# Where a modulation's weights are multiplied: 24 units of layer 1 move from the first block's heads to three norms of the second block

## The chip, the core and the metric

One core of a Trainium2 chip runs the whole program, in one launch. The metric is the device time of that launch in microseconds, as a median of runs. TensorE (PE) multiplies, VectorE (DVE) and ScalarE (ACT) do element-wise work on SBUF and PSUM, GpSimd (POOL) does one kind of subtraction here, and SyncE (SP) issues the loads of the weights.

## The reference, cut to what matters

Two transformer blocks of two layers each work on 256 tokens of width 1024, all in f32. The second block modulates its normed input by vectors that depend on a condition `c` alone:

```
mod_lat = silu(c) @ ada_w[l] + ada_b[l]          # 6 * 1024 columns
mod_ctx = silu(c_ctx) @ ada_w[l] + ada_b[l]
sh1, sc1, g1, sh2, sc2, g2 = split(mod, 6)
h = rmsnorm(x, norm1_g) * (1 + sc1) + sh1        # then mixer, then
x = x + g1 * out;  h2 = rmsnorm(x, norm2_g) * (1 + sc2) + sh2
x = x + g2 * conv_ffn(h2)
```

`ada_w` is two matrices of 1024 x 6144. Nothing in them waits for the first block, so their products can be made anywhere before the layer that uses them. The first block's attention has 24 heads (three mixers of eight) in each layer. The second block runs a context stream and a latent stream: layer 0 on the context, the keys and values of layer 1 on the context, then layers 0 and 1 on the latents.

## The kernel before, in words

All weights come as one stream of 908 units of 128 x 1024 f32 (512 KB), in the order in which PE uses them. `stream()` writes this order. SP loads unit i into one of seven `raw` buffers (L553) once unit i - 7 has left it. For an ordinary (split) unit ACT copies `raw` to a rounded `whi` (L1270, four buffers, a buffer is free when PE has used the unit four split units earlier), POOL computes the rest `wlo` (L568), and PE multiplies high by high, high by low and low by high (L599, L600, L603, or L616, L651 to L655 and L781 in other forms). A plain unit holds a 128-column tile of `ada_w` and isn't split: PE reads `raw` itself (L827) and the `raw` buffer is free when PE is done with it. Every engine walks the same stream by its own counter. ACT's counter runs four stream positions ahead of PE's, plain positions included; at a plain position `hi_part` does nothing.

`modulation_tile` (L827) multiplies one plain unit: eight f32 matmuls, each in two passes, whose 32-row outputs stand in four column groups of PE. The rows belong to the two conditions.

The 96 tiles of the two `ada_w` are spread over the first block. Of each layer's 48, 24 stand in `first_layer` beside the 24 heads, two ahead of the scores of each of the twelve pairs of heads (`pair_scores`). There DVE adds each tile's result to a running row in `lowest`, and twice a layer a matmul with a selecting matrix (L838, `modulation_columns`) turns twelve tiles' rows into columns and DVE adds the bias. The other 24 stand in three groups of eight in the layer's cross attention and in its two layer norms: there the eight accumulate in one PSUM tile of `lin`, ACT copies it once (`mod_row`), one L838 turns it (`unit_columns`) and `unit_bias` on DVE stores it and frees `lin` half 1. In the norms they lie between the small matmuls of the norm (`norm_with_modulation`), the last two in the chunk behind it (`columns_behind`).

Between the heads of a pair PE runs units of other projections (`first_fill`; `BEFORE_PV`, `AFTER_PV` say how many). ACT's program has at each pair: two copies of transposed probabilities, `hi_parts(2)`, the exponentials of the next pair, and then the steps of `first_fill`, each of them a `hi_part` and what must be evacuated.

The second block's norm is `rms()`, run five times: 1421, 1614, 1977, 2170 and 2484 us from the span's start. It follows the last matmuls of an output projection. DVE adds the residual in tiles, ACT squares them in five parts, PE sums the squares (L1120, L1124), DVE copies the sums (L1766), PE adds the parts (L1128), ACT takes the root (L1294), DVE the reciprocal (L1840), PE spreads it over the partitions (L770), DVE scales the first tile (L2246), ACT shifts and rounds it (L1574), and PE begins the next chunk (L616 for features, L668 for tokens). While PE would be idle there `keep_busy` gives it five bf16 matmuls on zeros (L1112), two ahead of L770 and three behind it.

Of the kernel before, what the change touches and what calls it, by code (L numbers as in the profile page):

```python
# [72 lines left out]
ADA_XA, ADA_LN_XA, ADA_LN_FFN = (6, 7), (8, 9), (10, 11)  # L73
# [30 lines left out]
def stream(v):  # L104
# [43 lines left out]
    for l in range(L):  # L148
        w_in = v["w_in"][l]
        ada = v["ada_w_2"][l]  # L150
        start = len(units)
        for j in range(3):
            chunk(w_in, A_COL + j * CH)
        chunk(w_in, B_COL)
        kr = w_in[:, B_COL + QL + KVL:C_COL]
        forget = np.pad(w_in[:, F_COL:GATE_COL], ((0, 0), (0, 64 - NH)))
        chunk(np.concatenate([w_in[:, B_COL + CH:B_COL + CH + P], forget, kr, kr[:, 16:], kr[:, :16]], -1), 0, kper=4, width=2 * P)
        chunk(w_in, C_COL)
        uq = v["b_w_uq"][l].reshape(QL, NH, 96)
# [30 lines left out]
        tiled = [(w, b) for w in ADA_XA for b in range(4)]  # L190
# [12 lines left out]
        units.extend(rows[1:])  # L203
        mixed.append(len(units))
        for c in ADA_LN_XA:
# [3 lines left out]
        for c in ADA_LN_FFN:  # L209
            modulation(ada, c * CH)  # L210
# [6 lines left out]
    def second(l):  # L217
# [18 lines left out]
        out(v["w_out_2"][l], KD)  # L236
        ffn_units(chunk, unit, paired["ffn_up_2"][l], v["ffn_down_2"][l])

    second(0)
    for c in range(4, 8):  # L240
        chunk(by_heads(v["w_in_2"][1]), c * CH)
    for l in range(L):
        second(l)
    split = [i not in plain for i in range(len(units))]
    for at in mixed:
        for kind in (units, split):
            kind[at:at + len(MIXED)] = [kind[at + i] for i in (EARLY if at == mixed[-1] else MIXED)]
# [30 lines left out]
def build(nc, a, split, n_first):  # L278
# [4 lines left out]
    with ExitStack() as ctx:  # L283
# [287 lines left out]
        def _(pe):  # L571
# [273 lines left out]
            def pair_scores(p):  # L845
# [3 lines left out]
                for g in heads:  # L849
                    modulation_tile(aux[:, g % 2, SW:CH], g % TURN, True, True)  # L850
# [28 lines left out]
            def pair_transposes(p):  # L879
# [3 lines left out]
                if (2 * p + 2) % TURN == 0:  # L883
                    pe.wait_ge(mod_row, t.next(mod_row))
                    modulation_columns(mod_out, mod_rows(2 * p), TURN)
                if p and 2 * p % TURN == 0:
# [118 lines left out]
            def first_layer(l, fill):  # L1005
# [10 lines left out]
                pair_scores(0)  # L1016
                advance(fill, 2)
                for p in range(PAIRS):
                    pair_transposes(p)
                    if p + 1 < PAIRS:  # L1020
                        pair_scores(p + 1)
# [3 lines left out]
                t.skip(mod_added, HEADS // TURN)  # L1025
# [89 lines left out]
            def rms():  # L1115
                for tiles in PARTS[:-1]:
# [89 lines left out]
            def second_layer(kts, rotate, start, stored=False):  # L1206
# [26 lines left out]
                rms()  # L1233
                ffn()
# [14 lines left out]
            second_layer(2, False, lambda: None)  # L1249
            rms()  # L1250
            token_chunk(0, fresh=TILES)
# [3 lines left out]
            for l in range(L):  # L1255
                second_layer(4, True, normed_chunk if l else lambda: feature_chunk(0, fresh=TILES), l == 1)

        @block.scalar
        def _(act):
# [154 lines left out]
            def first_layer(l):  # L1414
# [9 lines left out]
                hi_parts(2)  # L1424
# [3 lines left out]
                for p in range(PAIRS):  # L1428
                    for e in range(2):
                        transposed(SW, e)  # L1430
                    if p + 1 < PAIRS:
                        hi_parts(2)
# [143 lines left out]
            def rms(l, x, shift, then=None):  # L1576
# [5 lines left out]
                for k in range(KD):  # L1582
                    modulated_hi(l, shift, k)
                    if k == 3:
                        hi_part()
                if then:
                    act.preload_act_table(then)

# [53 lines left out]
            def second_layer(l, x, kts, rotate, normed=None):  # L1642
# [63 lines left out]
                rms(l, x, 24, ACT.Silu)  # L1706
# [20 lines left out]
            second_layer(0, context, 2, False)  # L1727
            rms(1, context, 0)
# [27 lines left out]
            second_layer(0, x, 4, True)  # L1756
# [3 lines left out]
        def _(dve):  # L1760
# [127 lines left out]
            def lowest(g):  # L1888
                if g == 0:
                    dve.wait_ge(bias_landed, t.next(bias_landed, 16))  # L1890
                lo_part()
# [4 lines left out]
                rows, new = mod_rows(g), aux[:, g % 2, SW:CH]  # L1896
                i = copy(rows, new) if g % TURN == 0 else tt_(rows, rows, new, ALU.add)
                if (g + 1) % TURN == 0:
                    i.then_inc(mod_row, 1)
# [132 lines left out]
            def first_layer(l):  # L2032
# [4 lines left out]
                lowest(0)  # L2037
                lowest(1)
# [4 lines left out]
                for p in range(PAIRS):  # L2043
                    if p + 1 < PAIRS:
                        lowest(2 * p + 2)
                        lowest(2 * p + 3)
# [5 lines left out]
                    if (2 * p + 2) % TURN == 0:  # L2052
# [35 lines left out]
                norm_with_modulation(l, "ln_xa", ADA_LN_XA)  # L2088
# [4 lines left out]
                norm_with_modulation(l, "ln_ffn", ADA_LN_FFN, not last)  # L2093
# [19 lines left out]
            def memory_heads(l):  # L2113
# [28 lines left out]
                modulation_bias(l, 4 * ADA_XA[0], late_columns, 8)  # L2142
# [278 lines left out]
            def second_layer(l, x, kts, rotate, coming=None, done=resid2):  # L2421
# [89 lines left out]
                rms_modulate(l, x, 1, 24)  # L2511
                if coming is not None:
# [9 lines left out]
            dve.memset(silc_wide[:, :], 0.0)  # L2522
            settle().then_inc(setup_done, 1)
# [42 lines left out]
            second_layer(0, context, 2, False, 1)  # L2566
            copy_shares()
            rms_modulate(1, context, 0, 0)
            for k in (2, 3):
# [7 lines left out]
            second_layer(0, x, 4, True, 0)  # L2577
# [90 lines left out]
```

## Time and profile before

| what | value |
| --- | --- |
| median of 3 runs | 2684.19 us (2682.64 to 2684.97) |
| the profiled execution's own time | 2683.82 us |
| its span, first to last instruction | 2681.9 us |
| PE busy, share of the span | 2656.8 us, 99% |
| ACT, DVE, POOL busy | 1425.3, 1158.5, 1940.0 us |
| HBM read | 489.27 MB, 184 GB/s over the span |

Busy time of PE is modelled: a matmul of 256 columns is told as 283 ns, while one starts every 0.12 us when they follow each other. So the times below are taken from start to start. Idle time in brackets at a row's end is that before the row, with the instruction that ended it. Several lines of the kernel are helpers (L599, L827, L838, L1287); the stretch of time tells which use of them is meant.

### The profile page before, as it was taken

Reading aid. Unit: us, or ns where it says so; the run is one execution under the profiler, and the core shown is the slowest. Engines: PE = TensorE matmul, PEld = TensorE weight load, DVE = VectorE, ACT = ScalarE, POOL = GpSimd, SP = SyncE. Lnnn points to the kernel's source line nnn. Section 1 sums busy time; section 2 is a strip of 40 time slices with the busy share of each in tenths; the row PEclk is TensorE's granted clock in tenths of the full one; section 3 lists DMA queues with packets and bytes.
Section 4 is the critical chain, followed back from the end, with each engine's and each line's share of the span. In section 5 each row is a group of like instructions: output and inputs, shape, how many; then the busy total and the mean of one; then the engine's idle time right before and its main releaser. Section 6 shows DMA issues by size and latency. Waiting matters only on the chain.

```text
span 2681.9 us, 48679 instructions
## 1 busy us (share of the span) xinstructions
PE 2656.8 (99%) x19951; PEld 2418.8 (90%) x19951; DVE 1158.5 (43%) x2323; ACT 1425.3 (53%) x2036; POOL 1940.0 (72%) x816
## 2 busy tenths in 40 slices
PE   8999999999999999999999999999999999999999
PEld 8899989989899899989998998888999988899898
DVE  2432342233324433434435554545345544542655
ACT  5656554446565544455654445556544455565443
POOL 6657658856567488687677886866678877567787
PEclk9999999999999999999999999999999999999999
DMA  7556475565565655564455555644445565335553
GB/s 280 198 194 215 157 247 186 188 234 191 189 220 197 219 191 188 191 220 160 150 165 167 191 186 178 210 149 134 150 158 192 186 216 180 128 132 173 165 186 129
DMA packets 137086, 495.59 MB, mean 185 GB/s; under 512 B 15136, under 2 KB 17440, under 8 KB 135968
## 3 DMA queue, kind: packets, MB, share of 16 engines
q1 hardware_dynamic: 132480, 480.55, 52.9%
q10 hardware_dynamic: 4384, 11.93, 1.3%
q8 instruction: 158, 2.59, 0.4%
q14 instruction: 64, 0.52, 0.1%
HBM read 489.27 MB, written 3.15 MB: 184 GB/s over the span
## 4 chain that ended last, share of the span: by engine, by line
PE 95%; ACT 2%; DVE 1%; DVEq 1%; issue 0%; ACTq 0%; DMA 0%; SPq 0%
PE lin L603 19%; PE lin L781 13%; PE lin L599 12%; PE lin L600 11%; PE aux L599 5%; PE aux L600 5%; PE aux L603 5%; PE lin L651 4%; PE lin L655 4%; PE lin L652 4%; PE aux L1163 2%; PE aux L1181 1%; PE aux L859 1%; PE aux L827 1%; PE lin L827 1%; PE aux L1170 1%
## 5 line engine op out<-in xcount | busy, mean ns | idle before, releaser
L568 POOL TENSOR_TENSOR wlo<-raw,whi 128x1024 fp32r<-128x1024 f32 x812 | 1939.8, 2408 | 731.6 <-ACT whi L1270 730.9
L1270 ACT ACTIVATE whi<-raw 128x1024 fp32r<-128x1024 f32 x812 | 845.2, 1057 | 635.3 <-PE lin L603 439.3
L603 PE MATMUL lin<-in_both,wlo 128*128 128x256 f32 x3520 | 500.2, 283 | 0.0
L599 PE MATMUL lin<-in_both,whi 128*128 128x256 f32 x1880 | 477.1, 291 | 11.0 <-ACT whi L1270 8.6
L603 PEld LDWEIGHTS lin<-in_both,wlo 128*128 128x128 f32 x3520 | 470.1, 192 | 15.6
L600 PE MATMUL lin<-in_both,whi 128*128 128x256 f32 x1880 | 463.9, 284 | 0.0
L781 PE MATMUL lin<-in_both,whi 128*128 128x512 f32 x1600 | 401.6, 393 | 0.6 <-DVEq L2209 0.4
L599 PEld LDWEIGHTS lin<-in_both,whi 128*128 128x128 f32 x1880 | 361.0, 192 | 43.7 <-issue 22.9
L600 PEld LDWEIGHTS lin<-in_both,whi 128*128 128x128 f32 x1880 | 361.7, 192 | 0.4
L781 PEld LDWEIGHTS lin<-in_both,whi 128*128 128x128 f32 x1600 | 287.6, 189 | 53.4 <-DVEq L2209 1.2
L2194 DVE TENSOR_REDUCE Z<-lin 128x512 f32<-128x1024 f32 x100 | 122.4, 1224 | 299.0 <-PE lin L603 297.7
L599 PE MATMUL aux<-br_hi,whi 128*128 128x256 f32 x880 | 219.1, 283 | 0.0
L600 PE MATMUL aux<-br_lo,whi 128*128 128x256 f32 x880 | 218.9, 283 | 0.0
L599 PE MATMUL lin<-br_hi,whi 128*128 128x256 f32 x768 | 195.5, 288 | 0.0
L600 PE MATMUL lin<-br_lo,whi 128*128 128x256 f32 x768 | 191.7, 283 | 0.0
L651 PE MATMUL lin<-whi,in_both 128*128 128x512 f32 x462 | 183.4, 397 | 0.3 <-DVE mods_all L1769 0.3
L652 PE MATMUL lin<-whi,in_both 128*128 128x512 f32 x462 | 180.2, 390 | 0.0
L599 PEld LDWEIGHTS aux<-br_hi,whi 128*128 128x128 f32 x880 | 168.9, 192 | 0.8 <-issue 0.8
L600 PEld LDWEIGHTS aux<-br_lo,whi 128*128 128x128 f32 x880 | 168.9, 192 | 0.0
L599 PEld LDWEIGHTS lin<-br_hi,whi 128*128 128x128 f32 x768 | 146.9, 191 | 6.8 <-issue 5.2
L600 PEld LDWEIGHTS lin<-br_lo,whi 128*128 128x128 f32 x768 | 147.1, 192 | 0.1
L603 PE MATMUL aux<-br_hi,wlo 128*128 128x256 f32 x880 | 134.9, 283 | 0.0
(284 smaller groups left out, 3560.7 us busy)
## 6 DMA issues: line engine op xcount, KB each, us to landing
raw<-in_wstream SPq DMA_DIRECT2D x908, 512.0 KB, 3.3
Z<-in_rel ACTq DMA_DIRECT2D x2, 1536.0 KB, 9.3
Z<-in_mem_t ACTq DMA_DIRECT2D x2, 1024.0 KB, 5.3
kv_store<-Z ACTq DMA_DIRECT2D x2, 1024.0 KB, 8.6
Z<-kv_store ACTq DMA_DIRECT2D x2, 1024.0 KB, 10.2
x<-in_x_t SPq DMA_DIRECT2D x2, 512.0 KB, 5.9
Z<-in_ctx_t SPq DMA_DIRECT2D x1, 1024.0 KB, 7.4
out_x<-x SPq DMA_DIRECT2D x4, 256.0 KB, 2.5
```

What stands on the lines that cost most here:

```text
L568: pool.tensor_tensor(wlo[s][:, :], raw[i % RAWS][:, :], whi[s][:, :].bitcast(F32), ALU.subtract).then_inc(lo_pool, 1)
L599: pe.matmul(out, wh, xh, start=start, stop=False, skip_group_check=True)
L600: pe.matmul(out, wh, xl, start=False, stop=False, skip_group_check=True)
L603: return pe.matmul(out, wl, xh, start=False, stop=stop, skip_group_check=True)
L651: pe.matmul(out, xh, wh, start=start, stop=False, skip_group_check=True)
L652: pe.matmul(out, xl, wh, start=False, stop=False, skip_group_check=True)
L655: return pe.matmul(out, xh, wl, start=False, stop=stop, skip_group_check=True)
L781: pe.matmul(lin[:, p, up * CH:(up + 1) * CH], wh[:, w], in_both[:, :, k * T:(k + 1) * T], start=(k == 0), stop=(k == KD - 1), skip_group_c ...
L827: mm = pe.matmul(out[j:j + 32], silc_wide[:, c:c + 32], w[:, k * P:(k + 1) * P], start=(first and k < 4), stop=(last and k >= 4), skip_gro ...
L1163: mm = pe.matmul(aux[:, m, 0:kts * P], q, head_keys(m, h, kts), start=True, stop=True)
L1270: act.activation(whi[s % SLOTS][:, :], raw[i % RAWS][:, :], ACT.Copy).then_inc(hi_ready, 1)
L2194: i = dve.tensor_reduce(three(u, 2), both.rearrange("p a (s t) -> p a t s", s=2), AX.X, ALU.add)
```

## The change

In `stream()`, layer 1 of the first block has no plain units among its heads. Its cross attention and its two layer norms, which held tiles 24 to 47 of `ada_w[1]`, now hold tiles 0 to 23, and tiles 24 to 47 are put into the stream ahead of three chunks of the second block, eight each, in the mixed order `MIXED` (four plain, then one split, one plain, one split, two plain, one split, one plain, one split). The three places are the norm ahead of the feed-forward of the context layer, the norm behind it (ahead of the keys of layer 1), and the norm ahead of the feed-forward of latent layer 0. The number of units, their bytes and the number of modulation tiles stay the same.

On PE, `pair_scores` and `pair_transposes` leave out the tiles, the two L838 and their two waits in layer 1. In the three norms `rms(fill)` has three tiles between the sums of squares, two in place of the first two `keep_busy` and one in place of the other three; the last two stand behind the first and second unit of the chunk that follows, and `unit_columns` behind its third. On ACT, `hi_parts(2)` ahead of the exponentials is gone in layer 1, and in the three norms four more `hi_part` come ahead of the squares, three behind tile 1 of the normed input and two behind tile 5 in place of the one behind tile 3; then ACT copies the row. On DVE, `lowest` leaves out the copy or the addition of a row in layer 1, `unit_bias` stands behind `rms_modulate` in the three norms, and one more `memset` (`mods_all`) stands in the setup.

```diff
@@ stream @@
+ADA = dict(xa=(6, 7), ln_xa=(8, 9), ln_ffn=(10, 11)), dict(xa=(0, 1), ln_xa=(2, 3), ln_ffn=(4, 5))
+ADA_CONTEXT, ADA_KEYS, ADA_LATENTS = (6, 7), (8, 9), (10, 11)
-        between_heads(dense, ada)
+        if l == 0:
+            between_heads(dense, ada)
+        else:
+            units.extend(dense)
...
+    def mixed_modulation(chunks):
+        mixed.append(len(units))
+        for c in chunks:
+            modulation(v["ada_w_2"][1], c * CH)
...
-    second(0)
+    second(0, ADA_CONTEXT)
+    mixed_modulation(ADA_KEYS)
     for c in range(4, 8):
         chunk(by_heads(v["w_in_2"][1]), c * CH)
-    for l in range(L):
-        second(l)
+    second(0, ADA_LATENTS)
+    second(1)
@@ tensor: pair_scores, rms, second_layer @@
-                for g in heads:
-                    modulation_tile(aux[:, g % 2, SW:CH], g % TURN, True, True)
+                if modulated:
+                    for g in heads:
+                        modulation_tile(aux[:, g % 2, SW:CH], g % TURN, True, True)
...
+                    if fill:
+                        advance(fill, (0, 2, 1, 0)[i])
...
-                pe.wait_ge(lin_free[0], t.ahead(lin_free[0]))
-                keep_busy(2)
-                spread_inverse(0)
-                keep_busy(3)
+                if fill:
+                    advance(fill, 2)
+                    spread_inverse(0)
+                    advance(fill, 1)
+                else:
+                    pe.wait_ge(lin_free[0], t.ahead(lin_free[0]))
+                    keep_busy(2)
+                    spread_inverse(0)
+                    keep_busy(3)
...
+                if modulated:
+                    fill = modulation_units()
+                    rms(fill)
+                    ffn(columns_behind(fill))
@@ scalar: first_layer, rms, second_layer @@
-                        hi_parts(2)
+                        if l == 0:
+                            hi_parts(2)
...
+            def modulation_row():
+                act.wait_ge(mod_used, n[0] - order[n[0]])
+                act.activation(ytok[:, 2 * P:3 * P], lin[:, 1, 0:P], ACT.Copy).then_inc(mod_row, 1)
...
-                    if k == 3:
+                    if modulated:
+                        hi_parts({1: 3, 5: 2}.get(k, 0))
+                    elif k == 3:
                         hi_part()
...
+                if modulated:
+                    hi_parts(4)
+                rms(l, x, 24, ACT.Silu, modulated)
@@ vector: lowest, second_layer @@
+                if modulated:
+                    rows, new = mod_rows(g), aux[:, g % 2, SW:CH]
...
+                if chunks:
+                    lo_parts(8)
+                    unit_bias(1, chunks[0])
```

## Rows read from the trace of the kernel before

**Rows 1.** The page: the chain that ended last, by engine.

```profile
PE 95%; ACT 2%; DVE 1%; DVEq 1%; issue 0%; ACTq 0%; DMA 0%; SPq 0%
```

**Rows 2.** Windows, L827 alone, over layer 1's heads: busy us (count), clock, DMA.

```profile
596.00:795.00 199.00, 12.97 (x384) 9.75 (x384) 1.00 0.56 202
```

**Rows 3.** Timeline of PE in those heads: start us, length us, engine, line, operation.

```profile
670.82 1.08 PE L827 MATMUL aux<-raw,silc_wide 128*32 128x128 f32 x32
671.83 1.58 PE L859 MATMUL aux<-Z 128*128 128x128 f32 x8
```

**Rows 4.** Timeline of ACT and PE at the wait inside layer 1's heads.

```profile
653.91 1.03 ACT L1385 ACTIVATE Z<-lin 64x1024 f32<-64x1024 f32 x1 [0.91 <-PE lin L603]
...
657.79 2.01 ACT L1270 ACTIVATE whi<-raw 128x1024 fp32r<-128x1024 f32 x2
659.82 1.28 ACT L1323 ACT_TABLE_LOAD   x1
...
663.14 1.02 ACT L1287 ACTIVATE Z<-lin 128x1024 f32<-128x1024 f32 x1
...
664.22 0.39 PE L599 MATMUL lin<-in_both,whi 128*128 128x256 f32 x1 [1.20 <-ACT Z L1287]
```

**Rows 5.** Windows, the first `rms`: PE, PEld, DVE, ACT, POOL busy us (count), clock, DMA share, GB/s.

```profile
1421.60:1427.00 5.40, 4.73 (x34) 2.39 (x32) 2.47 (x7) 2.02 (x6) 0.94 (x1) 1.00 0.43 145
```

**Rows 6.** Timeline of the first `rms`.

```profile
1421.70 1.71 PE L1120 MATMUL aux<-Z,c 128*32 128x256 f32 x14
...
1422.80 0.14 PEld L1120 LDWEIGHTS aux<-Z,c 128*32 128x32 f32 x2 [0.52 <-ACT Z L1580]
...
1423.46 0.42 DVE L1766 TENSOR_SCALAR probs<-aux 128x256 f32<-128x256 f32 x1 [0.77 <-PE aux L1120]
...
1423.93 0.61 PE L1128 MATMUL aux<-share,probs 128*128 128x1 f32 x4
...
1424.40 0.59 PE L1112 MATMUL lin<-zero_w 128*128 128x512 bf16 x2
...
1425.09 0.71 PE L770 MATMUL aux<-c,small 128*128 128x128 f32 x4
...
1426.98 0.36 PE L616 MATMUL lin<-in_both,whi 128*128 128x256 f32 x1 [0.53 <-ACT in_both L1574]
```

**Rows 7.** Timeline of PE in first-block norms and the chunks behind them.

```profile
360.32 1.52 PE L827 MATMUL lin<-raw,silc_wide 128*32 128x128 f32 x48
361.83 1.00 PE L756 MATMUL aux<-Z,c 128*32 128x256 f32 x6
...
570.90 0.64 PE L603 MATMUL lin<-in_both,wlo 128*128 128x256 f32 x4
571.47 0.64 PE L827 MATMUL lin<-raw,silc_wide 128*32 128x128 f32 x16
572.04 0.39 PE L599 MATMUL lin<-in_both,whi 128*128 128x256 f32 x1
...
578.65 0.29 PE L838 MATMUL lin<-c,ytok 128*128 128x16 f32 x2
578.79 0.36 PE L599 MATMUL lin<-in_both,whi 128*128 128x256 f32 x1
```

**Rows 8.** The page's DMA issues: line, count, KB each, us to landing.

```profile
raw<-in_wstream SPq DMA_DIRECT2D x908, 512.0 KB, 3.3
```

**Rows 9.** Timeline of PE, the first matmul behind two first-block norms.

```profile
367.83 1.03 PE L616 MATMUL lin<-in_both,whi 128*128 128x256 f32 x4 [1.18 <-ACT in_both L1311]
...
568.24 0.71 PE L616 MATMUL lin<-in_both,whi 128*128 128x256 f32 x4 [1.18 <-ACT in_both L1311]
```

**Rows 10.** Windows behind three first-block norms, columns as in rows 5.

```profile
368.10:371.30 3.20, 3.20 (x17) 3.20 (x17) 3.04 (x9) 1.87 (x3) 2.20 (x1) 0.50 1.01 410
...
568.30:571.50 3.20, 3.20 (x28) 2.93 (x30) 3.12 (x8) 2.08 (x4) 1.89 (x1) 1.00 1.02 410
927.90:931.10 3.20, 3.20 (x17) 3.20 (x17) 3.04 (x8) 1.64 (x3) 2.38 (x1) 0.50 1.05 421
```

More of the change, by code:

```diff
@@ L189, in stream @@
         del units[late:]
-        tiled = [(w, b) for w in ADA_XA for b in range(4)]
+        tiled = [(w, b) for w in ADA[l]["xa"] for b in range(4)]
         def adas(n):
@@ L204, in stream @@
         mixed.append(len(units))
-        for c in ADA_LN_XA:
+        for c in ADA[l]["ln_xa"]:
             modulation(ada, c * CH)
@@ L208, in stream @@
         mixed.append(len(units))
-        for c in ADA_LN_FFN:
+        for c in ADA[l]["ln_ffn"]:
             modulation(ada, c * CH)
@@ L215, in by_heads, with second @@
         return np.concatenate([w[:, :QK_COL], qk, w[:, V_COL:]], -1)
-    def second(l):
+    early = mixed[-1]
+    def mixed_modulation(chunks):
+        mixed.append(len(units))
+        for c in chunks:
+            modulation(v["ada_w_2"][1], c * CH)
+    def second(l, chunks=()):
         w_in = by_heads(v["w_in_2"][l])
@@ L246, in stream @@
         for kind in (units, split):
-            kind[at:at + len(MIXED)] = [kind[at + i] for i in (EARLY if at == mixed[-1] else MIXED)]
+            kind[at:at + len(MIXED)] = [kind[at + i] for i in (EARLY if at == early else MIXED)]
     return np.concatenate(units, 0), first, split
@@ L1113, in keep_busy, with rms @@
                               zero_w[:, :].unsqueeze(1).to_broadcast([P, 8, 64]), start=True, stop=True, skip_group_check=True)
-            def rms():
-                for tiles in PARTS[:-1]:
+            def rms(fill=None):
+                for i, tiles in enumerate(PARTS[:-1]):
                     pe.wait_ge(sq_ready, t.next(sq_ready))
@@ L1204, in branch_transposes, with second_layer @@
                         mm.then_inc(yb_trans, 1)
-            def second_layer(kts, rotate, start, stored=False):
+            def second_layer(kts, rotate, start, stored=False, modulated=False):
                 def first_scores():
@@ L1232, in second_layer @@
                 mixer_out()
-                rms()
-                ffn()
+                if modulated:
+                    fill = modulation_units()
+                    rms(fill)
+                    ffn(columns_behind(fill))
+                else:
+                    rms()
+                    ffn()
             pe.sem_inc(units_used, SLOTS)
@@ L1247, in latent_sums @@
                 group_squares(MG, 0, 4)
-            second_layer(2, False, lambda: None)
-            rms()
-            token_chunk(0, fresh=TILES)
+            second_layer(2, False, lambda: None, modulated=True)
+            fill = modulation_units()
+            rms(fill)
+            token_chunk(0, fresh=TILES, after=columns_behind(fill))
             token_chunk(1, after={2: lambda: qk_transposes(2)})
@@ L1574, in modulated_hi, with rms @@
                 act.activation(in_hi[:, k * T:(k + 1) * T], scaled_tile(k), ACT.Identity, bias=mod[l][:, shift + k:shift + k + 1]).then_inc(x_hi if k else first_hi, 1)
-            def rms(l, x, shift, then=None):
+            def modulation_row():
+                act.wait_ge(mod_used, n[0] - order[n[0]])
+                act.activation(ytok[:, 2 * P:3 * P], lin[:, 1, 0:P], ACT.Copy).then_inc(mod_row, 1)
+            def rms(l, x, shift, then=None, modulated=False):
                 for tiles in PARTS:
@@ L1726, in _ @@
             act.preload_act_table(ACT.Gelu_apprx_tanh)
-            second_layer(0, context, 2, False)
-            rms(1, context, 0)
+            second_layer(0, context, 2, False, modulated=True)
+            hi_parts(4)
+            rms(1, context, 0, modulated=True)
             qk_chunk(0, lambda: None)
@@ L1895, in lowest @@
                                              accum_out=stat(g, "minus")[:, tt:tt + 1])
[L1896 to L1899, printed above, removed]
+                if modulated:
+                    rows, new = mod_rows(g), aux[:, g % 2, SW:CH]
+                    i = copy(rows, new) if g % TURN == 0 else tt_(rows, rows, new, ALU.add)
+                    if (g + 1) % TURN == 0:
+                        i.then_inc(mod_row, 1)
                 settle().then_inc(maxed, 1)
@@ L2051, in first_layer @@
                     output_lo(p, 2)
-                    if (2 * p + 2) % TURN == 0:
+                    if l == 0 and (2 * p + 2) % TURN == 0:
                         modulation_bias(l, 2 * p + 2 - TURN, mod_out, TURN).then_inc(mod_added, 1)
@@ L2092, in first_layer @@
                 residual(lambda q: aux[:, q, :])
-                norm_with_modulation(l, "ln_ffn", ADA_LN_FFN, not last)
+                norm_with_modulation(l, "ln_ffn", ADA[l]["ln_ffn"], not last)
             def context_inverse():
@@ L2419, in diff_heads, with second_layer @@
                 settle()
[L2421 removed]
+            def second_layer(l, x, kts, rotate, coming=None, done=resid2, chunks=()):
                 dve.wait_ge(sgu_landed, t.next(sgu_landed, 48))
@@ L2522, in _ @@
             dve.memset(silc_wide[:, :], 0.0)
+            dve.memset(mods_all[:, :], 0.0)
             settle().then_inc(setup_done, 1)
@@ L2565, in _ @@
             dve.wait_ge(const2_landed, t.next(const2_landed, 16))
-            second_layer(0, context, 2, False, 1)
+            second_layer(0, context, 2, False, 1, chunks=ADA_CONTEXT)
             copy_shares()
             rms_modulate(1, context, 0, 0)
+            lo_parts(8)
+            unit_bias(1, ADA_KEYS[0])
             for k in (2, 3):
```

50 lines of the change are left out of this document (27 added, 23 removed).

## The prediction

> **What bounds the kernel.** I read the chain that ended last first: 95% of it is PE [rows 1]. So time goes where PE's stream gets shorter or longer, and where PE stands still. I then read windows and timelines at the two kinds of place the change touches.
>
> In layer 1's heads the modulation tiles are PE work like any other. The window has 384 passes of L827 [rows 2], 16 for a tile, so 24 tiles, which is all the change takes out. Two tiles run from 670.82 to 671.83, where the scores start [rows 3]: 1.01 us for a pair. The same distance stands at all twelve pairs of the layer. PE stands still once in these heads: at 664.22 it has idled 1.20 us for ACT's evacuation L1287 [rows 4]. There the heads are bound by ACT, not PE.
>
> In the second block's `rms` the reader is to see a chain that hops between engines: PE's sums, DVE's copy, PE's L1128, ACT's root, DVE's reciprocal, PE's L770, DVE, ACT, and PE's first product, 1421.70 to 1426.98 [rows 6]. In that window DVE, ACT and POOL are busy less than half the time and the DMA share is 0.43 [rows 5]; PE's 4.73 us hold `keep_busy`. All three stretches that are changed have this form and length, within 0.02 us.
>
> **What goes out of the heads.** 12 pairs x 1.01 = 12.12 us [rows 3]. The two column matmuls cost what L838 costs elsewhere, 578.65 to 578.79 [rows 7], 2 x 0.14 = 0.28. DVE's 24 small copies and additions go too; PE doesn't wait for them, so I count nothing.
>
> Not all of this arrives. The wait at 664.22 is set by ACT's program, and its order changes: two `hi_part` ahead of the exponentials go (2.01 us at 657.79 [rows 4]), but since ACT's counter runs four positions ahead, and these are now all split units, the same copies appear earlier and later. One now stands ahead of L1385, and both it and L1385 wait for the same PE unit, whose end started L1385 at 653.91. So L1385 and all behind it move back by one copy, 1.05 us; the pair at 657.79 is gone, -2.01; and the evacuation's own `hi_part`, empty before (a plain position), is now a copy, +1.05. ACT's L1287 comes at 663.14 + 1.05 - 2.01 + 1.05 = 663.2, counted from the scores before this wait. PE reaches the wait 1.01 us earlier and stands there 1.1 us longer. That pair of tiles gives nothing, and 0.1 us more is lost. The heads give 12.12 + 0.28 - 1.01 - 0.1 = 11.3 us. Bounds: 12.4 if ACT is not late there, about 9 if two more pairs hit such a wait. For the other pairs I see no evacuation within a microsecond of its use, and take 11.3.
>
> A rule of the Trainium skill bears on that chain: "ScalarE: Activation LUTs", section "What ACT_TABLE_LOAD costs", gives about 1.28 us for the load and 1.38 us more for a drain. The trace has a load of 1.28 us at 659.82 that begins 0.02 us behind the copies and is followed at once by the exponentials [rows 4], so it shows no drain. By the page ACT would be 1.4 us later and the heads would give 9.9; the row decides.
>
> **What comes into each of three norms.** Three tiles lie between the sums of squares. Before, tiles 0 to 3 of the squares are summed by about 1422.15, and PE then waits for ACT; the sum of tile 6 starts at 1422.80 [rows 6]. After: two tiles from 1422.16 to 1423.17 (1.01, rows 3), the sum of tiles 4 and 5 to 1423.6 (about 0.44, the larger part of the 0.66 us from tile 6's start to L1766, rows 6), one tile to 1424.1 (half of 1.01), then tile 6. It is 1.3 us late. DVE's copy L1766 and L1128 follow it directly, so they are 1.3 us late.
>
> Two tiles stand between L1128 and L770. L1128 to L770 takes 1.16 us before (1423.93 to 1425.09), bound by root and reciprocal, not by the zeros of L1112. After, PE needs 0.47 us for L1128 (as L1112 follows it at 1424.40), some 0.07 for the switch to L827, and 1.01 for the tiles: 1.55. So 0.39 us more. The sixth tile falls into the 1.89 us from L770 to L616 that DVE and ACT need anyway, and costs nothing. L616 is 1.69 us late.
>
> The chunk behind has no gap to hide in: its 24 matmuls of a unit run at 0.12 us. A lone tile there takes 571.47 to 572.04, 0.57 us [rows 7]; the last L603 before starts at 571.26, so 0.21 us pass instead of 0.12. Each costs 0.66, both 1.32. The column matmul costs 0.14 and the same switch, 0.23 us. Sum for one norm: 1.69 + 1.32 + 0.23 = 3.24 us; three: 9.72 us. As a check, three tiles in a row take 1.51 us [rows 7], so a tile costs 0.5 us there too. Bounds for one norm: 1.95, if only 0.4 us of the first 1.69 shows because the small matmuls overlap the tiles in other column groups, and 3.6 if none of the gaps is used as well as I think.
>
> **Queues.** In the mixed order seven units are loaded when `rms` begins, up to the second split one. The eighth, plain tile 5, can be issued when tile 0 is done (about 1422.9) and lands 3.3 us later [rows 8], about 1426.3; PE wants it near 1427.3. The third split unit follows the third tile's use, about 1424.3, and lands near 1428.8 if loads follow each other by 1.3 us (512 KB at 410 GB/s [rows 10]). ACT copies it after tile 1 of the input, near 1428.9, and holds up tiles 2 and 3 by some 0.55 us, which PE doesn't feel: its second unit is late by 0.66 on top. POOL gets it 5 us before PE needs it. `unit_bias` frees `lin` half 1 a whole unit before the next chunk wants it, and the layer parameters behind it on DVE fit in that unit. ACT waits for the eighth tile before its row copy; the next weight copy would have waited for a free buffer until about then. I count 0 for all of this. The new `memset` lies beside the first loads. POOL's work and the bytes don't change.
>
> **Sum.** -11.3 + 9.7 = -1.6 us. The profiled execution took 2683.82 us (1.9 around its span), 0.4 under the median of 2684.19, so I forecast 2682.2 for it and 2682.6 us for a median.
>
> **Rivals.**
>
> *The clock falls.* `keep_busy` goes. The trace shows what a hole can do: behind norms with tiles PE idled 1.18 us, and twice (368.1, 927.9) the granted clock was 0.50 (1.2 instead of 2.4 GHz) for over three microseconds, but once (568.3) 1.00 after the same hole [rows 9, 10]. PE did 17 matmuls in 3.2 us instead of 28, so a fall costs 11 x 0.12 = 1.3 us. For it: no zeros now stand behind L770. Against: a tile stands there, and tiles fill the earlier holes; the hole is, by my timeline, some 0.1 us longer than before. The widened wait in the heads (2.2 us instead of 1.2) is the likelier place. One to four falls: 2683.9 to 2687.8.
>
> *Better hidden.* The sums and roots absorb nearly all six tiles: 3 x 1.95 = 5.85 against 11.3 to 12.4, so -5.5 to -6.5, 2677.7 to 2678.7. For it: PE is idle for 0.67 us of the window and runs five matmuls on zeros in it [rows 5, 6]. Against: the tiles are put where only part of that idleness lies.
>
> *The weights come late (the slower side).* The third split unit can't be loaded before tile 2's buffer is free, and ACT, which is strictly in order, waits for it with input tiles 2 to 7 behind it. It decides once the unit lands more than about 6 us behind its issue, instead of 4.5: then PE's second unit waits. Other loads queued at 410 GB/s [rows 10] could do that. At 2.5 us a norm, -1.6 + 7.5 = +5.9: 2690.1. Against: the first block's norms have the same order of units and show no such wait.
>
> *The heads are not PE's.* If more pairs end in a wait for ACT, as the one in rows 4 does, only half of 11.3 arrives: +4.1, 2688.3.
>
> **Chances.** The forecast 0.55 (2680.5 to 2684.5), better hidden 0.14, the clock 0.15, late weights 0.08, the heads 0.08. The range goes from 2678.0 to 2687.5. 0.2% is 5.4 us, about what a measurement can tell from no change: faster than 2678.8 has 0.13, slower than 2689.6 has 0.08, the same 0.79.
>
> **What would show it.** Each pair of heads 1.01 us shorter; the idle time before that L599 about 2.2 us; L1120 to L616 near 6.9 instead of 5.3 us in three norms and unchanged in two; the clock 1.00 in them. A first chunk matmul waiting for ACT's `in_both` with ACT idle for a landing would prove me wrong, and so would a pair of heads that keeps its length.

## The result, and the profile after

The changed kernel took 2691.13 us (median of 19 runs, 2685.81 to 2696.48), the kernel before 2684.22 beside it. The ratio is 1.0025, 95% interval 1.0018 to 1.0031: 6.9 us slower, outside the range I gave (2678.0 to 2687.5) and beyond 2689.6, to which I had given 0.08. The runs of the changed kernel lie 10.7 us apart, those of the kernel before 3.1. The profiled execution took 2691.44 us, 7.6 more than the one before (2683.82).

I call the three changed norms (a), (b) and (c): ahead of the context's feed-forward, of the keys' chunk and of the latents' feed-forward. The page of the changed kernel, busy times:

```profile
PE 2656.6 (99%) x19938; PEld 2420.2 (90%) x19938; DVE 1172.0 (44%) x2301; ACT 1426.3 (53%) x2039; POOL 1940.9 (72%) x816
```

This says little. The waits of PE say more (us in total, times, longest; the first wait, for the first unit of all, is left out):

```profile
PE lin L795 <- DVE Z L2208: 4.8, 2, 3.7
PE aux L891 <- DVE br_lo L1811: 4.4, 1, 4.4
...
PE lin L613 <- ACT Z L1316: 1.2, 1, 1.2
PE lin L841 <- DMA raw<-in_wstream: 0.5, 1, 0.5
```

Both of the first two name DVE, and neither was there before. A wait is counted from the modelled end of the matmul ahead of it. Counted from when the next start was due, 0.12 us behind the last one, each is some 0.15 us longer: the 1.1, 3.7 and 4.4 us here are the 1.3, 3.9 and 4.6 us that the expectations below speak of. The wait for ACT in layer 1's heads [rows 4] is gone; what is left of that line is layer 0's.

To place the time I took the start of the first gate-and-up matmul in each of the five feed-forwards (layers 0 and 1 of the first block, then context, latents and last layer of the second) and the distances between them, minus those of the kernel before, one profiled run each. "wait (a), (b), (c)" is all from the first gate-and-up behind (a) to that behind (c), "wait (c)" from there to the one of the last layer. The kernels e1 to e10 are the experiments below:

```
             to ffn 0  heads of 1  norm (a)  wait (a), (b), (c)  wait (c)
predicted      0.0      -11.3        3.24        6.48              0.0
after          0.82      -9.75       3.02        7.84              5.96
e8, the same   0.82      -8.24       3.28       11.54              5.02
e1             0.14      -8.35       0.03       -0.02             -0.01
e2             0.44       0.30       3.03        7.69              1.52
e3            -0.24      -7.10       3.25        6.30             -0.12
e4            -1.58     -11.66       3.04        7.55              1.41
e5            -0.08     -10.47       3.03        7.19             -0.05
e6             0.30       0.27      -0.03        6.01              5.24
e7             0.19       0.00       0.01       -0.05             -0.04
e9            -1.59     -11.69       4.13        8.12              0.50
e10           -0.39     -10.51       6.67       15.48             -0.06
```

**Layer 1's heads.** Transposes now run straight into the scores, with no L841 between them; this is the pair that stood at 670.82 [rows 3]:

```profile
671.69 0.82 PE L891 MATMUL aux<-c,probs 128*128 128x128 f32 x6
672.35 1.48 PE L874 MATMUL aux<-Z 128*128 128x128 f32 x8
```

From one pair's scores to the next it is 1.0 to 1.6 us less than before in ten of the eleven distances. The eleventh is 4.3 us more: ahead of the fourth pair PE stands still. DVE, POOL and PE of the changed kernel there (start, length, engine, line, operation):

```profile
642.61 2.50 DVE L1989 TENSOR_SCALAR Z<-Z,par_all 8x256 f32<-8x256 f32 x1
645.19 2.46 DVE L1991 SCALAR_TENSOR_TENSOR Z<-Z 8x256 f32<-8x256 f32 x1
647.58 2.49 DVE L1992 TENSOR_SCALAR Z<-Z 8x256 f32<-8x256 f32 x1
...
651.25 2.43 DVE L1811 TENSOR_TENSOR Z<-Z 64x256 f32<-64x256 f32 x1
653.80 0.17 DVE L1948 RECIPROCAL small<-small 128x2 f32<-128x2 f32 x1
654.05 0.74 DVE L1951 TENSOR_SCALAR probs<-aux,small 128x128 f32<-128x128 f32 x2
```

```profile
642.20 7.73 POOL L582 TENSOR_TENSOR wlo<-raw,whi 128x1024 fp32r<-128x1024 f32 x3 [2.29 <-ACT whi L1299]
650.99 4.90 POOL L582 TENSOR_TENSOR wlo<-raw,whi 128x1024 fp32r<-128x1024 f32 x2 [1.07 <-ACT whi L1299]
```

```profile
656.07 1.33 PE L891 MATMUL aux<-c,probs 128*128 128x128 f32 x5 [4.41 <-DVE br_lo L1811]
```

The same in the kernel before, DVE and then POOL:

```profile
644.84 2.49 DVE L1945 TENSOR_SCALAR Z<-Z,par_all 8x256 f32<-8x256 f32 x1
647.42 0.42 DVE L1947 SCALAR_TENSOR_TENSOR Z<-Z 8x256 f32<-8x256 f32 x1
647.77 0.27 DVE L1948 TENSOR_SCALAR Z<-Z 8x256 f32<-8x256 f32 x1
...
649.23 0.42 DVE L1769 TENSOR_TENSOR Z<-Z 64x256 f32<-64x256 f32 x1
```

```profile
644.43 2.76 POOL L568 TENSOR_TENSOR wlo<-raw,whi 128x1024 fp32r<-128x1024 f32 x1 [2.29 <-ACT whi L1270]
651.18 4.75 POOL L568 TENSOR_TENSOR wlo<-raw,whi 128x1024 fp32r<-128x1024 f32 x2 [3.98 <-ACT whi L1270]
```

The reader is to see that operations of 0.27 to 0.42 us on 8 or 64 partitions take 2.4 to 2.5 us when they begin within a subtraction of POOL, and end when it ends. Before, three of these four fell into POOL's pause from 647.19 to 651.18. My reading is that POOL has that pause because two of ACT's `hi_part` there met positions of tiles and copied nothing. With the tiles out of the stream each is a copy, POOL has work from 642.2 to 649.9, and the divides behind the small operations are late. e4 below tests it. What is not slowed is as telling. At 653.80 POOL is at work again, and the reciprocal with one SBUF input takes its 0.17 us, L1951 with its input in PSUM its 0.74 for two (0.17 and 0.74 before, with POOL idle).

**The norms.** (a) from the first sum to the first product, PE alone (answers to rows 6):

```profile
1412.76 0.64 PE L1136 MATMUL aux<-Z,c 128*32 128x256 f32 x8
...
1417.43 0.71 PE L784 MATMUL aux<-c,small 128*128 128x128 f32 x4
...
1419.33 0.71 PE L630 MATMUL lin<-in_both,whi 128*128 128x256 f32 x4 [0.61 <-ACT in_both L1605]
```

6.57 us, 5.28 before: 1.29 more, where I had 1.69. (b) and (c) also take 6.57 us here. The granted clock stayed 1.00 in all three. The loss stands behind them. In (c), DVE, POOL and PE, then the window of the slow clock (columns as in rows 5):

```profile
1993.54 1.72 DVE L1808 TENSOR_SCALAR mod<-mods_all 128x48 f32<-128x48 f32 x1
1995.34 4.63 DVE L2277 SCALAR_TENSOR_TENSOR mscale<-mod,par_all 128x8 f32<-128x8 f32 x2
2000.06 1.45 DVE L2202 TENSOR_SCALAR Z<-lin,par_all 128x256 f32<-128x256 f32 x3
```

```profile
1992.82 9.47 POOL L582 TENSOR_TENSOR wlo<-raw,whi 128x1024 fp32r<-128x1024 f32 x4 [1.14 <-ACT whi L1299]
```

```profile
2000.79 1.00 PE L617 MATMUL lin<-in_both,wlo 128*128 128x256 f32 x7
2005.48 3.78 PE L795 MATMUL lin<-in_both,whi 128*128 128x512 f32 x8 [3.70 <-DVE Z L2208]
```

```profile
2004.30:2010.90 6.60, 5.42 (x17) 4.64 (x18) 5.01 (x9) 3.15 (x4) 2.35 (x2) 0.50 0.12 45
```

In the kernel before the same three operations stood at the end of `rms_modulate`, in a pause of POOL (idle for 2.89 us until 1991.12). DVE, then POOL:

```profile
1989.34 0.19 DVE L1766 TENSOR_SCALAR mod<-mods_all 128x48 f32<-128x48 f32 x1
1989.61 0.25 DVE L2233 SCALAR_TENSOR_TENSOR mscale<-mod,par_all 128x8 f32<-128x8 f32 x2
```

```profile
1991.12 4.79 POOL L568 TENSOR_TENSOR wlo<-raw,whi 128x1024 fp32r<-128x1024 f32 x2 [2.89 <-ACT whi L1270]
```

These layer parameters took 0.5 us there. Now they are behind `unit_bias`, in the chunk's last unit, where POOL is at work: 6.4 us. The convolution starts 4 us late, the second gate-and-up waits 3.7 us, and the clock is 0.50 (1.2 GHz) for 6.8 us, from 2004.2, inside that wait, to 2011.0. The convolution itself, SBUF on one side and PSUM on the other, runs at 0.48 us an operation beside the same POOL work.

### The profile page after: what moved, and what is told of

Read it like the earlier page. It is cut to its first block, busy times and chain, and to the rows that moved or that the text cites. A ratio compares the mean times of both kernels' runs of the same rounds, so it can differ in the third digit from the quotient of the medians.

```text
span 2689.5 us, 48633 instructions
## 1 busy us (share of the span) xinstructions
PE 2656.6 (99%) x19938; PEld 2420.2 (90%) x19938; DVE 1172.0 (44%) x2301; ACT 1426.3 (53%) x2039; POOL 1940.9 (72%) x816
## 4 chain that ended last, share of the span: by engine, by line
PE 95%; DVE 2%; ACT 1%; DVEq 1%; DMA 0%; issue 0%; ACTq 0%; SPq 0%
PE lin L617 18%; PE lin L795 13%; PE lin L613 12%; PE lin L614 11%; PE aux L613 5%; PE aux L614 5%; PE aux L617 5%; PE lin L665 4%; PE lin L666 4%; PE lin L669 4%; PE aux L1186 2%; PE aux L1204 1%; PE lin L841 1%; PE aux L874 1%; PE aux L1193 1%; PE aux L891 1%
## 6 DMA issues: line engine op xcount, KB each, us to landing
Z<-kv_store ACTq DMA_DIRECT2D x2, 1024.0 KB, 11.7
```

## The experiments

**e1_heads, e2_norms: the change in two halves.**

```
e1:  -    second(0, ADA_CONTEXT); mixed_modulation(ADA_KEYS) ... second(0, ADA_LATENTS)
     +    second(0) ... second(0)              # and rms(), token_chunk, ffn as before
e2:  -    if l == 0: between_heads(dense, ada) else: units.extend(dense)
     +    between_heads(dense, ada)            # and pair_scores, lowest, hi_parts(2) in both layers
```

> Only the heads' part of the change: layer 1's heads lose their 24 units, and the three norms stay as they were (the 24 units are in no other place, so the modulation values 0 to 23 of the second block's second layer are zero, and so are 24 to 47: this part of the computation is left out). Three theories. (A) VectorE is locked out: small VectorE operations that have both operands in SBUF wait out a GpSimd subtraction of 2.4 us, and in the heads that delayed the divides, so that TensorE idles 4.6 us near 651 and its clock falls once. Then the gain is the 8.9 us by which the start of the next feed-forward is earlier in the changed kernel: 2675.3 us (2674 to 2676.5). (B) My sum holds for the heads and the loss lies all in the norms: 11.3 us less, 2672.9. (C) The 24 units had cost TensorE less than 1.01 us a pair, the wait at 651 hides nothing: under 7 us less, above 2677.

> Only the norms' part: layer 1's heads keep their 24 units, and 24 units more are loaded and multiplied in the three norms, so the kernel has 24 units more than either of the two. (A) VectorE locked out by GpSimd, behind the norms (a) and (c), where the layer parameters now stand in the middle of GpSimd's work: 3.0 us for (a), then 7.8 us to the feed-forward of (c), then 6.0 us behind it, together 16.8: 2701 us (2699 to 2703). (B) My sum of 3.24 us for each norm: 9.7 us more, 2693.9. (C) The chip is slower from something that both parts share, as a lower clock without the heads' units: then the norms alone give 3.24 each and the heads alone give too little.

e1 took 2675.19 us, ratio 0.9965 (0.9952 to 0.9977): 9.4 less, as theory A had it; my 11.3 was not there, and the wait at 651 was (4.38 us). e2 took 2696.94, ratio 1.0045 (1.0032 to 1.0058): 12.4 more, between A (16.8, at least 14.5) and my 9.7, so neither has it. In the table its norm (a) costs 3.03, and what is above my sum lies in the waits behind (a) and (c), 1.36 and 1.41 us. (c)'s wait was shorter than in the changed kernel, and the reason can be read off DVE:

```profile
2003.07 1.74 DVE L1802 TENSOR_SCALAR mod<-mods_all 128x48 f32<-128x48 f32 x1
2004.89 2.34 DVE L2271 SCALAR_TENSOR_TENSOR mscale<-mod,par_all 128x8 f32<-128x8 f32 x2
```

Two operations in 2.34 us instead of 4.63: the second took 0.15, begun just as one subtraction ended. The halves add up to 3.0 us and the whole to 6.9, so something depends on how they meet.

**e3_params: the parameters later.**

```
-                if coming is not None:
-                    layer_params(1, coming)
-                ffn(l, True)
+                ffn(l, True, later=param_steps(1, coming) if coming is not None else ())
...
+                    if later and 6 <= c < 9:       # behind hidden(c)
+                        advance(later, 1)
```

> The changed kernel, with the layer parameters (the copy of 48 values and two operations on 8) taken out from behind the columns of each norm, one operation each behind the hidden chunks 6, 7 and 8 of the feed-forward, where VectorE has 2.5 us free. (A) VectorE locked out: the waits of TensorE at 1438 (1.3 us) and 2001 (3.9 us) go, and with the second the stretch of 6.8 us at half the clock (3.4 us): 8.6 us less than the changed kernel, 2682.5 us (2681.5 to 2684). (B) The convolution waits on something else (ScalarE's copies, the columns themselves): within 1.5 us of the changed kernel, 2690 to 2692.

2685.78 us, ratio to before 1.0004 (0.9995 to 1.0013): 5.4 less than the changed kernel, where A had 8.6 and B at most 1.5. Both waits are gone; the copy falls into a pause of POOL (2038.74 to 2040.10 in (c)) and takes 0.19 us, and the columns of (a) and of wait (c) are back at 3.25 and -0.12. The rest of what I expected was lost in the heads' stretch, where this trace has three falls of the clock (568, 657, 920) and the changed kernel's one.

**e4_lead: ACT's old positions in the heads.**

```
+            walk = []
+            for i in range(n_units + 8 * SLOTS):
+                walk.extend([(i, False)] * (2 * (i in places)))   # the 12 pairs' old places
+                walk.append((i, True))
...
-                i = n[0]
+                i, real = walk[n[0]]
...
-                if l == 0:
-                    hi_parts(2)
+                hi_parts(2)
```

> The changed kernel, with ScalarE's conversions in layer 1's heads at the positions they had before (it runs 2 to 4 units ahead, as when the 24 units stood there, and no longer always 4). TensorE's work is not changed. (A) VectorE is locked out because GpSimd is kept busy without a pause at 642 to 656: with the old positions the forget logits and the key's rotation take 0.3 to 0.5 us each again, TensorE's wait of 4.6 us at 651 and the fall of the clock behind it go, and the old wait of about 1.2 us for ScalarE's table at 663 comes back: 3.5 us less than the changed kernel, 2687.6 us (2686.5 to 2689). (B) The wait at 651 comes from TensorE being earlier, whatever ScalarE does: no difference, 2690 to 2692; or conversions that are late now hold TensorE and it is slower.

2688.64 us (2682.14 to 2693.82), ratio 1.0013 (1.0005 to 1.0022): 2.5 less than the changed kernel, in A's range. But its interval overlaps that of the changed kernel (1.0018 to 1.0031), so the time alone doesn't decide against B. The profiled run was its fastest, so the median can't be read off it, but the places can. DVE, POOL and ACT:

```profile
640.64 2.49 DVE L1997 TENSOR_SCALAR Z<-Z,par_all 8x256 f32<-8x256 f32 x1
643.22 0.41 DVE L1999 SCALAR_TENSOR_TENSOR Z<-Z 8x256 f32<-8x256 f32 x1
643.56 0.27 DVE L2000 TENSOR_SCALAR Z<-Z 8x256 f32<-8x256 f32 x1
```

```profile
640.22 2.77 POOL L584 TENSOR_TENSOR wlo<-raw,whi 128x1024 fp32r<-128x1024 f32 x1 [2.28 <-ACT whi L1309]
646.97 4.74 POOL L584 TENSOR_TENSOR wlo<-raw,whi 128x1024 fp32r<-128x1024 f32 x2 [3.98 <-ACT whi L1309]
```

```profile
653.61 2.01 ACT L1309 ACTIVATE whi<-raw 128x1024 fp32r<-128x1024 f32 x2
655.64 1.28 ACT L1362 ACT_TABLE_LOAD   x1
...
658.96 1.02 ACT L1326 ACTIVATE Z<-lin 128x1024 f32<-128x1024 f32 x1
```

```profile
660.04 0.39 PE L615 MATMUL lin<-in_both,whi 128*128 128x256 f32 x1 [2.21 <-ACT Z L1326]
```

POOL has its pause of 3.98 us back and the small operations their 0.27 to 0.41 us. The wait at 651 is gone, and the wait for ACT of rows 4 is back, 2.21 us long: the 1.20 from before and the 1.01 by which PE is earlier. That is what my step had said of it (2.2).

**e5_both.** e3 and e4 in one kernel.

> e3 and e4 together: the layer parameters behind the hidden chunks 6 to 8, and ScalarE's conversions in layer 1's heads at their old positions. (A) The two delays of VectorE are the whole of the loss that my sum lacks: the profiled run of e4 had the heads 11.9 us shorter at the first norm behind them, and each of the three norms costs 3.0 to 3.2 us (9.0 to 9.6), so 2684.5 - 11.9 + 9.3 = 2681.9 us (2680.5 to 2683), which is also what my sum of the prediction said (2682.6); its runs lie within 3 us, where those of e4 lay 11.7 us apart. (B) The spread of e4 comes from the heads or the clock and not from the parameters: a median of 2685 or more with a spread of over 6 us.

2682.50 us (2680.44 to 2685.98), ratio 0.9992 (0.9984 to 1.0001): 8.6 less than the changed kernel, 2.3 less than the kernel before beside it (2684.78), which can't be told from no change. A said 2681.9, my prediction 2682.6. The spread, 5.5 us, is half of the changed kernel's but not the 3 that I expected.

**e6_probe_sbuf, e7_probe_psum: the suspected cost by itself**, in the kernel before, without one unit moved. e7 differs in the first input only:

```
+                    third_done()                       # units_used of the chunk's third unit
+                    copy(scratch[:, 0:48], mods_all[:, 0:96:2])              # e7: inverse_out(0)[:, 0:96:2]
+                    settle()
+                    for i in range(2):
+                        dve.scalar_tensor_tensor(scratch[:, 48 + 8 * i:56 + 8 * i],
+                            mod[l][:, 8 * i:8 * i + 8], 1.0, par2("norm1", 1, 0, 8), ALU.add, ALU.mult)
+                        settle()                        # e7: inverse_out(0)[:, 8 * i:8 * i + 8]
```

> The kernel before, with none of the change, and three more operations of VectorE in each of the feed-forwards (a) and (c), issued once the third unit of its first chunk is used, where the changed kernel has the layer parameters: a copy of 48 values and two operations on 8 values with one input from each of two tiles, all in SBUF; their result is not used. (A) VectorE waits out GpSimd's subtractions: each of the three takes up to 2.4 us instead of 0.17 to 0.19, the convolution starts 2 to 6 us late and TensorE idles as long at the second gate-and-up, in both places, with a fall of the clock behind it: 2684.5 + 8 (4 to 14) = 2692 us. (B) Such operations cost their 0.2 us wherever they stand and the delay came from the modulation's columns or their wait: 2684.5, within 0.5.

> As e6, with the same three operations at the same place, but the first input of each is read from PSUM (the spread inverse, which lies there unused at that time); the output stays in SBUF. (A) With one operand in PSUM an operation does not wait for GpSimd (the convolution's operations between PSUM and SBUF took 0.48 to 0.54 us beside a running subtraction in the traces before and after): three times 0.2 to 0.3 us, done before the chunk is, TensorE doesn't wait: 2684.5, within 0.5. (B) It is the place, VectorE's queue or its second SBUF operand alone: the copy is quick and the two operations of 8 values with the gains as second input are slow, 3 to 5 us in all.

e6 took 2696.46 us, ratio 1.0042 (1.0028 to 1.0056), 11.7 more for six operations of forms that cost 0.2 us each when POOL is idle. A had 4 to 14 more, B nothing. The waits behind (a) and (c) are 3.93 us each, and the clock falls at both (for 6.8 and 3.4 us). e7 took 2683.59, ratio 0.9997 (0.9988 to 1.0006). DVE behind (a) in e6, then POOL and PE:

```profile
1436.42 2.15 DVE L1766 TENSOR_SCALAR probs<-mods_all 128x48 f32<-128x48 f32 x1 [1.46 <-PE lin L603]
1438.64 4.63 DVE L2522 SCALAR_TENSOR_TENSOR probs<-mod,par_all 128x8 f32<-128x8 f32 x2
```

```profile
1436.11 9.48 POOL L568 TENSOR_TENSOR wlo<-raw,whi 128x1024 fp32r<-128x1024 f32 x4 [2.90 <-ACT whi L1270]
```

```profile
1448.77 1.65 PE L781 MATMUL lin<-in_both,whi 128*128 128x512 f32 x3 [3.93 <-DVE Z L2167]
```

and DVE and POOL in e7:

```profile
1436.08 0.21 DVE L1766 TENSOR_SCALAR probs<-aux 128x48 f32<-128x48 f32 x1 [1.46 <-PE lin L603]
1436.37 0.41 DVE L2522 SCALAR_TENSOR_TENSOR probs<-aux,par_all 128x8 f32<-128x8 f32 x2
```

```profile
1435.77 9.51 POOL L568 TENSOR_TENSOR wlo<-raw,whi 128x1024 fp32r<-128x1024 f32 x4 [2.90 <-ACT whi L1270]
```

Same place, same POOL work, 0.7 us instead of 6.8. So it is not DVE's queue and not the wait for the columns. With their inputs in SBUF these operations wait for POOL's running subtraction; with the first input in PSUM they do not.

The Trainium skill says this in "SBUF — State Buffer", section "Who interferes with whom": VectorE and GpSimd share one pair of ports as an exclusive lock, held for a whole instruction. A VectorE operation contends for it with a GpSimd instruction that reads SBUF if it has two SBUF inputs, and also if it is a copy or `tensor_scalar` in a two-port mode. The rows of e6 (2.15 and 4.63 us), e7 (0.21 and 0.41) and the heads (2.43 to 2.50) agree with it. The section doesn't name the reciprocal, which has one SBUF input and kept its 0.17 us.

**e8_again: the changed kernel once more.**

> The changed kernel once more, for a second trace. (A) Whether the second and third parameter operation slip in between two subtractions (a gap of about 0.05 us) or wait out one more decides 2.4 us each time and a fall of the clock: the wait of TensorE at the feed-forward of (c) is either about 1.5 us, as in e2 and e4, or about 3.9, as in the changed kernel's first trace; time between 2686 and 2696. (B) The wait at (c) is the same 3.9 us again, and the spread comes from other places.

2695.8 us, one run. The wait behind (c) was 3.69 us again, so there B is right; but behind (a) it was 3.69 too, where the first trace of the same program had 1.14. DVE behind (a), first trace and then e8:

```profile
1431.81 2.22 DVE L2277 SCALAR_TENSOR_TENSOR mscale<-mod,par_all 128x8 f32<-128x8 f32 x2
```

```profile
1433.85 4.51 DVE L2277 SCALAR_TENSOR_TENSOR mscale<-mod,par_all 128x8 f32<-128x8 f32 x2
```

The second operation either falls between two subtractions or pays for a whole one, 2.4 us. In both outcomes it begins within 0.01 us of POOL's next subtraction by the profile's times (1433.87 and 1433.88 in the first trace, both 1435.93 in e8). That this is a race which small shifts decide is my reading of such pairs in the changed kernel, e8, e2 and e4; what shifts them I haven't shown.

**e9_spread, e10_all: could the norm be cheaper?** e5, with the units placed as my sum says they should be:

```
-                        advance(fill, (0, 2, 1, 0)[i])
+                        advance(fill, (0, 1, 0, 0)[i])          # e10: (0, 2, 0, 0)
...
+                    advance(fill, 1)                            # ahead of the wait for shares_ready
...
-                    advance(fill, 1)
+                    advance(fill, 3)                            # behind spread_inverse
-   {0: lambda: advance(fill, 1), 1: lambda: advance(fill, 1), 2: unit_columns}
+   {0: lambda: advance(fill, 1), 2: unit_columns}               # e10: {2: unit_columns}
```

> e5 with the eight units of each norm placed otherwise: one behind the second pair of sums (was two, and one behind the third), one while VectorE copies the shares, two ahead of the spread as before, three behind it (was one), one in the chunk (was two). (A) As my sum priced a norm (the roots 1.3 us later for three units among the sums, 0.39 for one more, 0.66 for each lone unit in the chunk), two units less in front of the roots give 0.6 to 1.0 us and one lone unit less 0.66: 1.3 to 1.6 us for each of three norms less than e5, so 2678.5 us (2677.5 to 2680). (B) The norm is bound by ScalarE and VectorE behind the spread, and a unit put there delays the first product as much as it saves: 2682 to 2683 as e5. (C) The last units have not landed when they are wanted, and each norm gets 0.5 to 1 us dearer.

> As e9, with two units behind the second pair of sums and none in the chunk, so all eight ahead of the first product. (A) One more among the sums costs 0.3 to 0.5 us there and saves 0.66 in the chunk: 0.2 us a norm less than e9, 2678 us. (C) The eighth unit's load has not landed by the end of the spread (in e5 the sixth came 0.1 us ahead of its use and loads land 1.3 us apart, so the eighth comes 2.6 us later): TensorE waits 1 to 2 us in each norm, 2681 to 2684.

Both missed towards C. e9 took 2686.30 us (2683.65 to 2694.11), ratio 1.0009 (1.0000 to 1.0018); e10 2695.36, ratio 1.0038 (1.0025 to 1.0052). The waits of PE in e9:

```profile
PE lin L843 <- DMA raw<-in_wstream: 4.1, 4, 1.4
```

In each norm of e9 PE waits 1.2 to 1.4 us at the 7th unit for its load, and in (a) and (c) of e10 3.2 and 2.9 us at the 8th, with a fall of the clock at each of its three norms. So more than six units ahead of the first product run into the rate at which loads land. The placement of the change, with two units left for the chunk, was the better one.

## Why the prediction was wrong

*What comes out of the heads, 11.3 us: the size held, a step was missing.* With ACT's old positions the stretch is 11.7 us shorter (e4, one fall of the clock in it, as before). In the changed kernel it is 9.8 and 8.2 in its two traces. The step that failed is "Not all of this arrives": I followed the change of ACT's order into the one wait that existed and counted 0.1 us for it (no run shows that 0.1: in the changed kernel PE comes too late for this wait, and e4's 2.21 us, with the old order, are 1.20 and 1.01), but not into POOL, which gets its work from the same copies, and from POOL into DVE. I wrote that "for the other pairs I see no evacuation within a microsecond of its use", and looked only at evacuations. What stood there instead is the wait of 4.41 us ahead of the fourth pair, where I had 2.2 to 2.3 us at the old place.

*What comes into a norm, 3.24 us: held.* 3.02 to 3.28 for (a) in six traces. The parts were off in opposite directions: 1.29 instead of 1.69 us to the first product, and 1.7 instead of 1.55 in the chunk. For (b) and (c) together the two kernels without the wait behind (a), e3 and e5, give 6.3 and 7.2 against 6.48. The 0.9 us between them isn't in a norm: at 1674.8 and 1677.2 of e5 PE waits 0.22 us for a copy of ACT and 0.31 for POOL behind it, after ACT had issued loads until 1673.5, and there PE falls back 1.1 us against e3.

*The queues, 0 us: this step failed.* "`unit_bias` frees `lin` half 1 ... and the layer parameters behind it on DVE fit in that unit." They do by the durations that they had (0.5 us), and those were taken from a place where POOL was idle. In the new place they take 3.9 (6.4 in e8) and 6.4 us. I said "POOL's work and the bytes don't change", and they don't; its timetable does. That costs 1.3 us behind (a) and 6.0 behind (c) in the first trace, and 6.0 and 5.2 in e6, where nothing of the change is left but these operations. A row that contradicted me stood in the trace before: 2.49 us for L1945 on 8 x 256 at 644.84, with 0.27 for the same form at 647.77.

*The rivals.* None was the one. "The clock" had falls, but as a consequence: those of layer 1's heads and behind (c) stand at the holes that DVE made (655.9, 2004.2) or at the ACT wait that I had named (660.7 in e4). None stands in a norm without `keep_busy`, but for e10's, which have their waits for loads. "Late weights" is true at its edge (0.49 us in (b)) and would have counted with one more unit up front, as e9 shows. Its 2690.1 lies near the measured time by chance. "The heads are not PE's" has the right place and the wrong engine.

*The sum.* In the first trace: 0.8 us ahead of the change (the fall of the clock is at 147, in layer 0's heads, and at 368 in the kernel before; the change has no part in it), 1.6 of the heads, 1.4 behind (a) and in (b), 6.0 behind (c), 0.2 and 0.3 given back in norm (a) and at the end: 9.2 over my -1.6, which makes the 7.6. With both delays of DVE removed the median is 2682.50, 0.1 from my forecast. That it is so close is in part luck: in e5's trace the heads give 10.5 instead of 11.3 and what lies behind them costs 10.2 instead of 9.7, and its profiled run took 2683.34, 1.1 over what I had forecast for one. What stays open is the spread of e4 and e9 (11.7 and 10.5 us): it goes with the granted clock (0.999 in the fastest, 0.995 and 0.996 in the slowest), but I have traces of their fast runs only.

## What to carry to other kernels

Take an operation's duration from a place with the neighbours that it will have, not from where it stands now: here 0.2 us became 2.4 because GpSimd was at work beside it, and a small VectorE operation on the path should read from PSUM, or stand where GpSimd pauses. When work is removed, follow not only the engine that gets shorter but every engine that it paced: the empty positions of the tiles were what gave GpSimd its pause. And a sum that comes out at nothing (-1.6 of 2684 us) leaves no room for a step that was only said to fit.

## What the runs showed that I had not expected

- Six VectorE operations of 0.2 us cost 11.7 us of 2684 where GpSimd is at work (e6), and nothing that can be told if the first input comes from PSUM (e7).
- The blocked operation waits for the end of the running subtraction and not for a share of it, and each of a series pays again: 2.15, then 4.63 us for two, unless it slips in between two subtractions. The loss goes the other way as well: POOL's subtraction at 644.43 before took 2.76 us instead of 2.40, having begun while an all-SBUF subtraction of DVE (to 644.93) was running.
- The same program had 1.14 or 3.69 us of wait at the same place in two runs.
- A reciprocal of two values a partition, SBUF to SBUF, kept its 0.17 us beside POOL, and so did the copies of a single value (0.14).
- At each of the ten holes of PE of over 3 us in these traces, but for the one ahead of the first product, the granted clock fell to 0.50 for 3.4 or 6.8 us, from 1.7 us before the hole's end (e6 at 1447.1) to 1.6 us behind it (e10 at 1422.0). At holes of 1.2 to 1.4 us it sometimes did [rows 10] and sometimes not (e2 at 2012.7), and a few falls have no hole ahead of them that I could name (147 in the changed kernel, 707 in e2).
